# One core, two-layer hybrid decoder trunk: the SBUF tensors are allocated in another order

## The chip, the cores and the metric

The kernel runs on one core of a Trainium2 chip. The metric is the device time of one execution in microseconds; less is better. Before the change the median of three runs is 1443.9 us (1442.6 to 1444.5).

## The reference

The reference is a trunk of two layers over 512 tokens of width 1024, all in float32. Cut to what matters:

```python
for l in range(DEPTH):                                   # DEPTH = 2
    h = rmsnorm(x, norm_g[l]) * (1.0 + scale) + shift     # scale, shift, gate from silu(c) @ w_mod[l]
    parts = split_cols(h @ w_in[l])                       # 1024 -> 7200 columns
    y_a = hgrn2_mixer(...) * silu(a_g)                    # 4 heads of 128
    y_b = mla_mixer(c_q, c_kv, k_rope, ...) * silu(b_g)   # 8 heads; c_q (768) and c_kv (256) are normed first
    y_c = retention_mixer(...) * silu(c_g)                # 4 heads of 128
    merged = (sigmoid(m_a) * (y_a @ w_pa[l]) + sigmoid(m_b) * (y_b @ w_pb[l])
              + sigmoid(m_c) * (y_c @ w_pc[l]))
    x = x + gate * (merged @ w_out[l])
return rmsnorm(x, final_g)
```

## The kernel before

Everything is kept transposed: a tile is 128 features (the partitions) by 512 tokens, 2 KiB in each partition. A loop over the two layers holds one long list of steps, written out for each engine; semaphores tie the engines together.

**The stream of weights.** The weights of a layer come as 93 items of at most 128 x 1024 elements, through a ring of three slots. SP loads an item into `raw` (L548). ScalarE (ACT) copies it, rounded to the matmul format fp32r, into `w_hi` (L839). GpSimd (POOL) subtracts and puts the rest into `w_lo` (L576). The other operand of each product is likewise held as two tensors, a rounded part and a rest. So each 128x128 block of weights gives three matmuls with 512 columns, all into one accumulator in PSUM. `wh` and `wl` are the blocks that stay in the array (stationary), `hi` and `lo` the tiles that stream through it (moving):

```python
nc.tensor.matmul(dst[0:m, :], wh, hi, start=(k == 0), stop=False)
nc.tensor.matmul(dst[0:m, :], wh, lo, start=False, stop=False)
last = nc.tensor.matmul(dst[0:m, :], wl, hi, start=False, stop=(k == nk - 1))
```

These are lines 663 to 665 (`item`), and lines 648 to 650 for the first two items of a layer (`first_items`). In the rows of the profile the moving operand is named first and the stationary one second: `ps_st<-h_hi,w_hi`. There are five kinds of moving operand, chosen in `moving`:

- `h_hi`, `h_lo`: the normed input of the layer, for all columns of `w_in`. These are tensors of their own.
- `cq_hi`, `cq_lo`, `ckv_hi`, `ckv_lo` (MLA's up-projections), `y_hi`, `y_lo` (the outputs of HGRN2 and MLA, for `w_pa` and `w_pb`), `yc_hi`, `yc_lo` (retention, for `w_pc`), `mg_hi`, `mg_lo` (the merged sum, for `w_out`). These lie in the region that the stages share, the arena.

The mixers' own matmuls (scores, values, transposes, column sums) are plain float32, not fp32r.

**SBUF.** A partition of SBUF is one row of bytes. `sb(name, shape)` allocates the next tensor behind the one before. The arena is 92 KiB; `at(name, offset, ...)` places a tensor at a fixed offset from its start, and tensors of different stages lie over one another there. Every offset is a multiple of 1 KiB. Before the change the arena stands behind everything else.

**Ahead of the loop** ScalarE's queue loads 16 pieces of `w_mod_first` into `pro_w` in the arena, VectorE (DVE) folds them into `pro_acc`, and `x` is loaded by SP.

The functions and lines that the change touches:

Of the kernel before, what the change touches and what calls it, by code (L numbers as in the profile page):

```python
# [33 lines left out]
P = 128  # L34
D_MODEL, SEQ, DEPTH = 1024, 512, 2
DT = D_MODEL // P
# [344 lines left out]
def build(nc, x_t, positions, cst, decay, params_cur, params_nxt, w_stream, w_mod, w_mod_first, out_t):  # L381
    ctx = ExitStack()
    with ctx:
        def sb(name, shape, dt=F32):
            return ctx.enter_context(nc.sbuf_tensor(name, shape, dt))
# [2 lines left out]
            return ctx.enter_context(nc.semaphore(name))  # L388


        x = sb("x", [P, DT, SEQ])
        h_hi = sb("h_hi", [P, DT, SEQ], F32R)
        h_lo = sb("h_lo", [P, DT, SEQ], F32R)
        raw = sb("raw", [P, RING, SLOT])
        w_hi = sb("w_hi", [P, RING, SLOT], F32R)
        w_lo = sb("w_lo", [P, RING, SLOT], F32R)
# [20 lines left out]
        carry = sb("carry", [P, 1])  # L417
        neg_max = sb("neg_max", [P, CH])


        arena = nc.sbuf_base + (-nc.sbuf_base) % 64
        KB = 1024

        def at(name, offset, shape, dt=F32):
            return nc.alloc_sbuf_tensor_at(name, shape, dt, offset=arena + offset)


        hg_q, hg_k, hg_b = at("hg_q", 0, [P, 2, SEQ]), at("hg_k", 4 * KB, [P, 2, SEQ]), at("hg_b", 8 * KB, [P, 2, SEQ])
        hg_e, hg_x = at("hg_e", 12 * KB, [P, 2, SEQ]), at("hg_x", 16 * KB, [P, 2, SEQ])
        hg_at = (at("hg_at0", 20 * KB, [P, CH, SEQ]), at("hg_at1", 40 * KB, [P, CH, SEQ]))  # L430
        hg_kd = at("hg_kd", 28 * KB, [P, 3 * P])
        hg_qc = at("hg_qc", 64 * KB, [P, 3, 3 * P])
        hg_vt = at("hg_vt", 69 * KB, [P, SEQ])
        hg_v = at("hg_v", 71 * KB, [P, 2, CH, P])
# [22 lines left out]
        merged = at("merged", 32 * KB, [P, DT, SEQ])  # L457
        y_hi, y_lo = at("y_hi", 48 * KB, [P, CH, SEQ], F32R), at("y_lo", 56 * KB, [P, CH, SEQ], F32R)
        sigma = at("sigma", 84 * KB, [P, 3, SEQ])
        arena_end = arena + 92 * KB  # L460
        assert arena_end <= nc.sbuf_usable_end, (arena_end, nc.sbuf_usable_end)
        mg_hi, mg_lo = at("mg_hi", 0, [P, DT, SEQ], F32R), at("mg_lo", 16 * KB, [P, DT, SEQ], F32R)

        pro_w = at("pro_w", 0, [P, PRO_RING, D_MODEL])
# [1217 lines left out]
```

## Time and profile before

| | |
|---|---|
| median of 3 runs | 1443.9 us (1442.6 to 1444.5) |
| the profiled execution, its own time | 1443.96 us |
| its span in the trace | 1442.2 us |
| PE (matmul) busy | 1323.3 us, 92% |
| DVE, ACT, POOL busy | 758.0, 641.3 and 601.4 us |
| mean granted TensorE clock | 0.978 of full speed |

Matmuls overlap one another in the trace: one takes some 390 ns from start to end, while the next one starts some 230 ns after it. So a busy PE does not tell how fast the stream of matmuls runs; the distance from one start to the next does, and it is read from a list of instructions in order of time.

### The profile page before, as it was taken

What the parts mean: (1) busy time and instruction counts of PE and PEld (TensorE: products, weight loads), DVE (VectorE), ACT (ScalarE), POOL (GpSimd) and SP (SyncE); (2) the same over time, 40 slices, a digit from 0 to 9 for tenths busy, and PEclk for the clock granted to TensorE, in tenths of its full rate; (3) what the DMA queues carried; (4) which work ended last, traced back from release to release, by engine and by line L of the source; (5) the groups of instructions that cost most, each with busy time, mean ns of one, the idle gap of its engine ahead of it and who ended that gap; (6) DMA issues with size and microseconds to landing.
All of it is one profiled execution on the core that took longest, in us unless ns stands there. A gap on an engine that the chain in (4) does not pass through costs nothing.

```text
span 1442.2 us, 20431 instructions
## 1 busy us (share of the span) xinstructions
PE 1323.3 (92%) x5886; PEld 1040.6 (72%) x5886; DVE 758.0 (53%) x1174; ACT 641.3 (44%) x988; POOL 601.4 (42%) x756
## 2 busy tenths in 40 slices
PE   0389889999999999999978988999999999999996
PEld 0177677888777777778856777778877777778884
DVE  6877876533455424433337787653346541444333
ACT  2245544544455334444334555455445533444531
POOL 3243333464323444545534332346432344445451
PEclk9999999999999999999988999999999999999998
DMA  9132212244223233333323222224422223333331
GB/s 368 38 102 74 70 55 89 83 136 125 79 72 94 86 106 106 88 105 110 89 76 109 72 61 61 92 83 133 131 74 74 84 99 98 104 91 111 101 97 59
DMA packets 46057, 140.06 MB, mean 97 GB/s; under 512 B 5744, under 2 KB 5744, under 8 KB 45680
## 3 DMA queue, kind: packets, MB, share of 16 engines
q1 hardware_dynamic: 28656, 102.65, 23.6%
q10 hardware_dynamic: 17280, 35.99, 7.8%
q8 instruction: 52, 0.85, 0.2%
q14 instruction: 69, 0.57, 0.1%
HBM read 136.52 MB, written 2.10 MB: 96 GB/s over the span
## 4 chain that ended last, share of the span: by engine, by line
PE 78%; DVE 12%; issue 4%; ACT 4%; DMA 1%; ACTq 1%; DVEq 0%
PE ps_st L663 21%; PE ps_st L665 21%; PE ps_st L664 21%; PE ps_o L685 4%; PE ps_s L755 2%; PE ps_s L710 2%; PE ps_s L779 1%; PE ps_w L764 1%; DVE pro_acc L1131 1%; PE ps_misc L680 1%; DMA pro_w<-w_mod_first 1%; DVE hg_x L1340 1%; DVE h_lo L1400 1%; DVE gate_x L1190 1%; PE ps_misc L671 1%
## 5 line engine op out<-in xcount | busy, mean ns | idle before, releaser
L576 POOL TENSOR_TENSOR w_lo<-raw,w_hi 128x256 fp32r<-128x256 f32 x744 | 588.3, 822 | 793.9 <-ACT w_hi L839 793.5
L663 PE MATMUL ps_st<-h_hi,w_hi 128*128 128x512 f32 x1008 | 416.5, 413 | 0.7 <-POOL w_lo L576 0.4
L665 PE MATMUL ps_st<-h_hi,w_lo 128*128 128x512 f32 x1008 | 398.6, 395 | 0.0
L664 PE MATMUL ps_st<-h_lo,w_hi 128*128 128x512 f32 x1008 | 398.2, 395 | 0.0
L663 PEld LDWEIGHTS ps_st<-h_hi,w_hi 128*128 128x128 f32 x1008 | 193.3, 192 | 48.9 <-issue 8.3
L664 PEld LDWEIGHTS ps_st<-h_lo,w_hi 128*128 128x128 f32 x1008 | 192.7, 191 | 44.6 <-issue 6.2
L665 PEld LDWEIGHTS ps_st<-h_hi,w_lo 128*128 128x128 f32 x1008 | 192.1, 191 | 41.8
L839 ACT ACTIVATE w_hi<-raw 128x1024 fp32r<-128x1024 f32 x186 | 195.2, 1050 | 29.9 <-PE ps_st L665 27.5
L861 ACT ACTIVATE gate_t<-gate_x 128x512 f32<-128x512 f32 x80 | 50.6, 632 | 242.2 <-DVE gate_x L1190 242.2
L1190 DVE TENSOR_SCALAR gate_x<-ps_st 128x512 f32<-128x512 f32 x80 | 55.2, 690 | 193.0 <-PE ps_st L665 191.4
L710 PE MATMUL ps_s<-hg_x 128*128 128x128 f32 x384 | 54.4, 292 | 28.7 <-DVE hg_x L1340 28.7
L1538 DVE SCALAR_TENSOR_TENSOR mod_acc<-mod_w,cond,mod_acc 128x512 f32<-128x512 f32 x84 | 71.3, 848 | 10.0
L710 PEld LDWEIGHTS ps_s<-hg_x 128*128 128x128 f32 x384 | 49.9, 203 | 34.2 <-issue 19.9
L863 ACT ACTIVATE gate_t<-gate_t,cs 128x512 f32<-128x512 f32 x80 | 57.9, 724 | 2.6
L663 PE MATMUL ps_st<-y_hi,w_hi 128*128 128x512 f32 x128 | 51.1, 399 | 0.0
L664 PE MATMUL ps_st<-y_lo,w_hi 128*128 128x512 f32 x128 | 50.6, 395 | 0.0
L665 PE MATMUL ps_st<-y_hi,w_lo 128*128 128x512 f32 x128 | 50.5, 395 | 0.0
L665 PE MATMUL ps_st<-mg_hi,w_lo 128*128 128x512 f32 x128 | 50.5, 394 | 0.0
L663 PE MATMUL ps_st<-mg_hi,w_hi 128*128 128x512 f32 x128 | 50.4, 394 | 0.0
L664 PE MATMUL ps_st<-mg_lo,w_hi 128*128 128x512 f32 x128 | 50.4, 394 | 0.0
L589 PE MATMUL ps_misc<-cs,pro_acc 128*128 128x1 f32 x32 | 7.1, 352 | 46.1 <-DVE pro_acc L1131 46.1
L1256 DVE SCALAR_TENSOR_TENSOR x<-ps_st,gate,x 128x512 f32<-128x512 f32 x16 | 12.0, 750 | 63.1 <-PE ps_st L665 63.1
(233 smaller groups left out, 1987.9 us busy)
## 6 DMA issues: line engine op xcount, KB each, us to landing
raw<-w_stream SPq DMA_DIRECT2D x186, 512.0 KB, 3.6
mod_w<-w_mod ACTq DMA_DIRECT2D x96, 256.0 KB, 2.7
pro_w<-w_mod_first ACTq DMA_DIRECT2D x16, 512.0 KB, 12.7
x<-x_t SPq DMA_DIRECT2D x4, 512.0 KB, 10.5
ret_decay<-decay ACTq DMA_DIRECT2D x2, 1024.0 KB, 4.9
out_t<-o_t SPq DMA_DIRECT2D x8, 256.0 KB, 2.2
cs<-cst SPq DMA_DIRECT2D x1, 906.5 KB, 5.2
pos_i<-positions ACTq DMA_DIRECT2D x1, 256.0 KB, 7.3
```

The lines of the kernel that those rows point to most:

```text
L576: ins = nc.gpsimd.tensor_tensor(w_lo[:, i % RING, r], raw[:, i % RING, r], w_hi[:, i % RING, r].bitcast(F32), ALU.subtract)
L663: nc.tensor.matmul(dst[0:m, :], wh, hi, start=(k == 0), stop=False)
L664: nc.tensor.matmul(dst[0:m, :], wh, lo, start=False, stop=False)
L665: last = nc.tensor.matmul(dst[0:m, :], wl, hi, start=False, stop=(k == nk - 1))
L685: last = nc.tensor.matmul(dst[:, k * P:], values(k), weights[:, k, k * P:], start=(k == 0), stop=(k == CH - 1))
L710: last = nc.tensor.matmul(dst[:, r], left[:, r], right[:, r], start=True, stop=True)
L755: nc.tensor.matmul(dst[:, 0:w], mla_q[0:96, h % 2, qi * P:w], mla_kv[0:96, h % 2, 0:w], start=True, stop=False)
L839: A(w_hi[:, i % RING, 0:n], raw[:, i % RING, 0:n], ACT.Copy).then_inc(w_hi_ready, 1)
L861: A(t_n, x_n, ACT.Exp, scale=-1.0).then_inc(act_link, 1)
L863: A(t_n, t_n, ACT.Ln, bias=one).then_inc(act_link, 1)
L1190: V.tensor_scalar(gate_x[:, n % 2, :], bank[bank_of((it, 0))][:], SIG_MIN, None, ALU.max)\
L1538: ins = V.scalar_tensor_tensor(mod_acc[:], mod_w[:, n % 2, :], cond[:, k:k + 1], mod_acc[:], ALU.mult, ALU.add)
```

## The change

Only the places of the tensors in SBUF change. The list of instructions, their operands, their waits and their order are the same, word for word, on all five engines. The diff:

```diff
@@ build()
-        x = sb("x", [P, DT, SEQ])
+        KB = 1024
         h_hi = sb("h_hi", [P, DT, SEQ], F32R)
         h_lo = sb("h_lo", [P, DT, SEQ], F32R)
+        arena = nc.sbuf_base + (-nc.sbuf_base) % 64
+        sb("arena_room", [P, 92 * KB // 4 + 16])
+        x = sb("x", [P, DT, SEQ])
         raw = sb("raw", [P, RING, SLOT])
         w_hi = sb("w_hi", [P, RING, SLOT], F32R)
         w_lo = sb("w_lo", [P, RING, SLOT], F32R)
@@
         neg_max = sb("neg_max", [P, CH])
-        arena = nc.sbuf_base + (-nc.sbuf_base) % 64
-        KB = 1024
@@
-        arena_end = arena + 92 * KB
-        assert arena_end <= nc.sbuf_usable_end, (arena_end, nc.sbuf_usable_end)
```

The room for the arena is 92 KiB and 64 bytes more. The addresses in a partition that follow from the two orders, in bytes (1152 bytes are taken ahead of the first tensor in both), and their remainders by 128 and by 256, which hold for every piece of the tensor that is a multiple of 256 bytes from its start:

| tensor | before | rest by 128, by 256 | after | rest by 128, by 256 |
|---|---|---|---|---|
| `h_hi`, `h_lo` | 17536, 33920 | 0, 128 | 1152, 17536 | 0, 128 |
| the arena, 92 KiB | 133952 to 228160 | 64, 64 | 33920 to 128128 | 0, 128 |
| `x` | 1152 | 0, 128 | 128192 | 64, 192 |
| `raw`, `w_hi`, `w_lo` | 50304, 62592, 74880 | 0, 128 | 144576, 156864, 169152 | 64, 192 |
| `mod_w`, `mod_acc`, `cs` | 87168, 91264, 93312 | 0, 128 | 181440, 185536, 187584 | 64, 192 |
| `rstd`, `gate_t`, `sq_sum` | 112352, 118496, 130784 | 96, 224 | 206624, 212768, 225056 | 32, 32 |

Before the change all of the arena lies above 131072 (128 KiB), and `h`, `x`, the weights' ring and the constants below it. After it the arena and `h` lie below that address, and the weights' ring and what follows above. These two parts are called the lower and the upper half here.

## Rows read from the trace of the kernel before

**Rows 1.** The page: busy time of each engine, PE's tenths and granted clock in 40 slices
```profile
PE 1323.3 (92%) x5886; PEld 1040.6 (72%) x5886; DVE 758.0 (53%) x1174; ACT 641.3 (44%) x988; POOL 601.4 (42%) x756
...
PE   0389889999999999999978988999999999999996
...
PEclk9999999999999999999988999999999999999998
```

**Rows 2.** The page: the chain that ended last, shares by engine and by line
```profile
PE 78%; DVE 12%; issue 4%; ACT 4%; DMA 1%; ACTq 1%; DVEq 0%
PE ps_st L663 21%; PE ps_st L665 21%; PE ps_st L664 21%; PE ps_o L685 4%; PE ps_s L755 2%; PE ps_s L710 2%; PE ps_s L779 1%; PE ps_w L764 1%; DVE pro_acc L1131 1%; PE ps_misc L680 1%; DMA pro_w<-w_mod_first 1%; DVE hg_x L1340 1%; DVE h_lo L1400 1%; DVE gate_x L1190 1%; PE ps_misc L671 1%
```

**Rows 3.** Windows of the first layer: window, its length, busy us (count) of each engine, PEclk, DMA share, GB/s
```profile
70.00:240.00 170.00, 153.00 (x707) 123.58 (x707) 134.19 (x231) 85.78 (x142) 66.63 (x76) 0.94 0.26 77
240.00:300.00 60.00, 58.75 (x260) 47.04 (x259) 30.82 (x44) 30.83 (x49) 29.37 (x36) 1.00 0.33 101
300.00:365.00 65.00, 65.00 (x286) 52.98 (x285) 18.42 (x24) 26.09 (x35) 35.22 (x49) 1.00 0.42 126
365.00:500.00 135.00, 134.50 (x637) 102.10 (x636) 73.25 (x121) 67.78 (x119) 42.82 (x57) 1.00 0.28 83
500.00:620.00 120.00, 120.00 (x508) 91.28 (x507) 44.76 (x67) 49.45 (x70) 53.66 (x68) 1.00 0.33 99
620.00:745.00 125.00, 121.96 (x531) 98.54 (x530) 45.79 (x63) 48.15 (x66) 59.06 (x80) 1.00 0.32 94
```

**Rows 4.** Line 663, its instructions: count, duration in ns (min/median/max), first and last start
```profile
L663 PEld LDWEIGHTS ps_st<-h_hi,w_hi x1008: 186/188/337, 81.3 to 1376.5; 128*128 128x128 f32 x168
L663 PE MATMUL ps_st<-h_hi,w_hi x1008: 387/389/988, 81.3 to 1376.7; 128*128 128x512 f32 x168
...
L663 PE MATMUL ps_st<-y_hi,w_hi x128: 393/394/497, 298.7 to 1314.5; 128*128 128x512 f32 x128
...
L663 PE MATMUL ps_st<-mg_hi,w_hi x128: 393/394/395, 696.8 to 1427.1; 128*128 128x512 f32 x128
...
L663 PE MATMUL ps_st<-cq_hi,w_hi x96: 393/394/484, 331.7 to 1136.5; 128*128 128x512 f32 x96
...
L663 PE MATMUL ps_st<-yc_hi,w_hi x64: 393/394/395, 646.2 to 1382.3; 128*128 128x512 f32 x64
...
L663 PE MATMUL ps_st<-ckv_hi,w_hi x32: 393/394/399, 335.9 to 1137.9; 128*128 128x512 f32 x32
```

**Rows 5.** PE in order of time, matmuls with `h` moving: start us, duration us
```profile
304.32 0.39 PE L663 MATMUL ps_st<-h_hi,w_hi 128*128 128x512 f32 x1
...
305.48 0.39 PE L665 MATMUL ps_st<-h_hi,w_lo 128*128 128x512 f32 x1
305.70 0.39 PE L663 MATMUL ps_st<-h_hi,w_hi 128*128 128x512 f32 x1
...
309.78 0.39 PE L663 MATMUL ps_st<-h_hi,w_hi 128*128 128x512 f32 x1
```

**Rows 6.** The same, with `mg` moving: the first and the last of `w_out`'s 192 in layer 1
```profile
696.78 0.39 PE L663 MATMUL ps_st<-mg_hi,w_hi 128*128 128x512 f32 x1
...
741.34 0.40 PE L665 MATMUL ps_st<-mg_hi,w_lo 128*128 128x512 f32 x1
```

**Rows 7.** Line 680, plain float32 column sums, their instructions as in Rows 4
```profile
L680 PE MATMUL ps_misc<-o_sq,cs x32: 590/592/692, 134.8 to 1315.6; 128*128 128x512 f32 x32
...
L680 PE MATMUL ps_misc<-sq_sum,cs x8: 590/692/1220, 58.0 to 955.4; 128*128 128x512 f32 x8
```

**Rows 8.** Lines 791 and 685, weight loads of plain float32, as in Rows 4
```profile
L791 PEld LDWEIGHTS ps_w<-cs,mod_acc x96: 187/192/193, 179.7 to 1355.2; 128*128 128x128 f32 x96
...
L685 PEld LDWEIGHTS ps_o<-ret_sc,ret_v x64: 187/190/192, 530.7 to 1303.9; 128*128 128x128 f32 x64
```

**Rows 9.** Groups by line and form: count, busy us, mean ns, idle before and its releaser
```profile
L576 POOL TENSOR_TENSOR w_lo<-raw,w_hi 128x256 fp32r<-128x256 f32 x744 | 588.3, 822 | 793.9 <-ACT w_hi L839 793.5
...
L874 ACT ACTIVATE sigma<-gate_t 128x512 f32<-128x512 f32 x48 | 30.3, 632 | 4.8
...
L1152 DVE TENSOR_TENSOR mg_lo<-merged,mg_hi 128x512 fp32r<-128x512 f32 x16 | 10.4, 689 | 1.0
...
L944 ACT ACTIVATE sq_t<-x 128x512 f32<-128x512 f32 x16 | 10.1, 632 | 67.4 <-DVE sq_sum L1283 61.7 <-DVE x L1256 5.7
...
L1231 DVE TENSOR_TENSOR sq_sum<-sq_sum,sq_t 128x512 f32<-128x512 f32 x10 | 6.9, 689 | 28.0 <-ACT sq_t L908 28.0
```

**Rows 10.** DMA queues, 8 to 20 us: packets, MB, share of the 16 engines' time
```profile
q10 hardware_dynamic: 657, 2.43, 50.6%
q1 hardware_dynamic: 658, 2.40, 50.5%
```

## The prediction

> **What bounds the kernel now.** I read the page first: PE is busy 1323.3 of 1442.2 us, and its tenths stand at 9 nearly everywhere but at the two starts of a layer [rows 1]. The chain that ended last is PE for 78%, and 63% of it is the three matmul lines of `item` [rows 2]. The windows say where PE is the only limit: from 300 us to the end of the layer it is busy 65.00 of 65, 134.50 of 135 and 120.00 of 120 us; the loss of 3.0 us between 620 and 745 is the turn to the next layer. Only between 70 and 240 us, where HGRN2 runs beside it, does PE lose 17 of 170 us [rows 3]. The clock is not in question: it is at its upper level in all of these windows but the first, where 0.94 of it is granted [rows 3]. So what this kernel pays for is the distance from one fp32r matmul to the next, and an allocation can move the time only if that distance, or a wait in the HGRN2 stage, depends on where an operand lies.
>
> Does it? The same line, with the same weights' ring as stationary operand and the same 512 columns, shows two durations. With `h` moving the median is 389 ns; with `y`, `mg`, `cq`, `yc` and `ckv` moving it is 394 ns each time, and nearly without spread (393 to 395 for `mg` and `yc`) [rows 4]. The distances say the same more sharply. From 305.70 to 309.78 us there are 18 steps with `h` moving: 4.08/18 = 0.2267 us. From 696.78 to 741.34 us there are 191 steps with `mg` moving: 44.56/191 = 0.2333 us [rows 5, 6]. That is 6.6 ns more, and the weights, the engine and the shape are the same. What differs is the place of the moving tensor: `h` stands at a rest of 0 by 128 and in the lower half of the addresses, the arena at a rest of 64 and in the upper half (table of the change). I cannot tell from this trace which of the two it is. For the moving operand I need not: after the change the arena has the rest of `h`, by 128 and by 256, and lies in the lower half, and `h` keeps its rest and its half.
>
> **The change part by part.**
> No instruction is added, removed or moved, so each term is a count times a difference in duration.
>
> (a) Moving operands in the arena. Line 663 has 128 + 128 + 96 + 64 + 32 = 448 of them [rows 4], and lines 664 and 665 as many each: 1344. If they come down from 0.2333 to 0.2267 us that is 1344 x 0.0066 = -8.9 us. They lie in the stretches from 298 to 743 us and the same of layer 2, where PE is busy all the time [rows 3], so none of it is hidden. A part may not be had: with `h` moving too, the first steps behind a change of operand or a wait are longer (304.32 to 305.48 us, 5 steps, 0.232 each [rows 5]). The 16 items of MLA's up-projections begin behind a step of the attention, so some 6 of each one's 24 may gain nothing: 16 x 6 x 0.0066 = +0.6. On the other side the slow first steps of `h` behind an arena item would go (5 x 0.005 us, some 15 times: -0.4). Sum -8.7.
>
> (b) The stationary operands. `w_hi` and `w_lo` go from a rest of 0 by 128 to 64, and from the lower to the upper half. The fp32r stream has no row with them elsewhere. The nearest rows are weight loads. One takes 188 ns in the stream [rows 4], against a step of 227, so some 39 ns are in hand; a penalty of 6.6 ns as for a moving operand would lie inside that. So the lower bound is 0. The upper bound is that the penalty shows in full wherever it does not now: then all 3120 matmuls with `h` (1008 x 3 [rows 4] and 96 of the first items) go to 0.2333, 3120 x 0.0066 = +20.6 us, less the quarter that runs at 0.23 already (6 of 24 steps, [rows 5]): +15.5. I take 0, because the load has room and because the difference that is seen goes with the moving tensor's name and never with the slot of the ring.
>
> (c) Plain float32 matmuls. The column sums with `o_sq` (arena) and with `sq_sum` (below the arena, rest 96) both have a shortest duration of 590 ns [rows 7]. A weight load from `mod_acc`, below, takes 187 to 193 ns and one from `ret_v`, in the arena, 187 to 192 [rows 8]. I take 0; the bound is some 2 ns on about 1400 of them, 3 us to either side, half of it hidden.
>
> (d) ScalarE and VectorE. The same activation of 128x512 takes 632 ns from `x` (rest 0, lower half) and from `gate_t` into `sigma` (rest 96 into the arena) [rows 9]. VectorE takes 689 ns for two tiles of 512 both at a rest of 96 (`sq_sum`) and in the arena (`mg_lo`) [rows 9]. No sign of an address: 0.
>
> (e) GpSimd. Its four subtractions of an item read `raw` and `w_hi` and write `w_lo`, all three of which move. There is no row for them elsewhere. But GpSimd idles 793.9 us in front of them, all of it waiting for ScalarE [rows 9]; 6 ns on each of 744 would be 4.5 us of busy time and nothing in the end: 0. If they took 10% longer (82 ns), the ring would still be ahead: 3.3 us of work per item against some 5.4 us of matmuls (24 x 0.227).
>
> (f) DMA. Between 8 and 20 us queue 1 fills `x` and `raw` (rest 0) and queue 10 `pro_w` (rest 64 by 128), side by side: 2.40 MB for 50.5% and 2.43 MB for 50.6% [rows 10], the same price to 1%. So swapping their rests costs nothing; in the prologue, which waits for `pro_w` and where VectorE and GpSimd get in each other's way, I allow 1 us to either side.
>
> The sum against the profiled execution: 1443.96 - 8.7 = 1435.3 us. That execution is at the median of the runs (1443.9), so the forecast for the median is **1435.2 us**; this case's own range is 1433.5 to 1437.5, from (a) without its losses and (f) on one side to half of (c) on the other.
>
> A page speaks against any effect. The Trainium skill, "TensorE: Matmul & The Clock Gate", section "Back-to-back issue gap", gives the gap as columns over clock plus 2.5 ns and knows no address in it. By it the time would not change. The row says that the gap is 227 for one tensor and 233 for others at one column count, so here the measurement decides. The same section says that in a stream of weight loads and matmuls the spacing is set by both; that speaks for the rival below. "Step-by-step: what each phase is for" on the same page gives the moving and the stationary operand a read port each, which speaks against it; no row here shows the ports.
>
> **The rivals.**
> *The stationary operand counts as well: slower.* The place is lines 648 to 650 and 663 to 665 with `h` moving. Today both operands are at a rest of 0 for `h`, and they differ for the arena. After the change moving and stationary differ everywhere (rests 128 and 192 by 256; today's `y` and `w_hi` are 64 and 128, the same difference). If the longer step comes from that difference, or if each misplaced operand costs a step of 6.6 ns, `h` rises to 0.2333 and the arena stays there: +15.5 us as in (b), some of it taken by the HGRN2 stage's waits, 1459 us. For it: the step with `h` moving needs some six matmuls to settle at 0.2267 [rows 5], which looks like two streams finding their distance rather than a fixed price per address. Against it: the 39 ns of room, and that weight loads themselves take the same time wherever they read [rows 8]. It decides from the point where the step with `h` rises by more than 1344/2340 of the arena's gain, that is by 3.8 ns.
>
> *No effect: 1444.* The arena's tensors would have to be slow for another reason than their place, say by what wrote them or what runs beside them. `mg` is written by ScalarE and VectorE as `h` is, and the steps are 0.2333 in a stretch without any mixer beside it, so I see little for it.
>
> *Only a part: 1439 or so.* The step with the arena moving would stop midway, if two conditions added up, the rest and the half, and one of them were undone by what moved up with the weights.
>
> **How the numbers follow.** Moving operand alone: 0.58. The stationary one as well: 0.28. No effect, or changes that cancel: 0.08. A part: 0.06. About 0.2% (2.9 us) is what a measurement of this kernel can tell from no change. Faster takes the first and the last, 0.64; slower the second with a little of the third, 0.28; the rest, 0.08, is within 0.2%. The two signs share most of the chance, so the range reaches from the likeliest case to the rival: 1433 to 1460, with 1433.5 to 1437.5 for the likeliest case alone.
>
> **What would show it.** Line 663 in the profile after: a median of 389 ns for `y`, `mg`, `cq`, `yc`, `ckv` and a step of 0.2267 for `mg` show (a) right. 389 ns for `h` as before shows (b) right; 394 for `h` shows the rival, and 394 for all of them its full form. A weight load longer than 188 with `h` still at 0.2267 would show the room of 39 ns used. GpSimd's mean of 822 ns and the packets' shares answer to (e) and (f). The prediction is wrong if the 512-column step with `h` moves at all, or if PE begins to wait for `w_lo`.

## The result, and the profile after

The change makes the kernel slower: 1455.94 us (median of 6 runs, 1454.78 to 1456.57) against 1443.63 us (6 runs, 1441.55 to 1444.5), a ratio of 1.0088 with a 95% interval of 1.0076 to 1.0099. The forecast was 1435.2 us and faster. The time lies in the forecast's range, at the rival that had 0.28.

The page after, busy times, with its span of 1454.8 us (before: [rows 1]):

```profile
span 1454.8 us, 20431 instructions
...
PE 1338.1 (92%) x5886; PEld 1041.6 (72%) x5886; DVE 756.3 (52%) x1174; ACT 641.4 (44%) x988; POOL 601.5 (41%) x756
...
PEclk9999999999999999999988999999999999999998
```

PE is busy 14.8 us longer with the same 5886 matmuls, at the same granted clock; no other engine moved by more than 2 us. The windows, with columns as in [rows 3], show the same: PE is as busy as before, with fewer matmuls in the same stretch (499 against 508 between 500 and 620 us).

```profile
300.00:365.00 65.00, 65.00 (x282) 52.44 (x281) 18.94 (x25) 26.46 (x35) 35.31 (x49) 1.00 0.41 123
...
500.00:620.00 120.00, 120.00 (x499) 89.99 (x499) 43.93 (x66) 47.72 (x67) 53.71 (x68) 1.00 0.34 99
```

Line 661 is what was line 663 ([rows 4]): count, duration in ns (min/median/max), first and last start.

```profile
L661 PEld LDWEIGHTS ps_st<-h_hi,w_hi x1008: 186/188/337, 81.0 to 1389.5; 128*128 128x128 f32 x168
L661 PE MATMUL ps_st<-h_hi,w_hi x1008: 392/394/988, 81.1 to 1389.7; 128*128 128x512 f32 x168
...
L661 PE MATMUL ps_st<-y_hi,w_hi x128: 393/394/503, 300.2 to 1326.4; 128*128 128x512 f32 x128
...
L661 PE MATMUL ps_st<-mg_hi,w_hi x128: 393/396/398, 703.0 to 1440.1; 128*128 128x512 f32 x128
```

With `h` moving the duration went from 389 to 394 ns; with the arena's tensors it did not come down; the weight load is at 188 ns as before. The distances, from PE in order of time:

```profile
636.57 0.40 PE L662 MATMUL ps_st<-h_lo,w_hi 128*128 128x512 f32 x1
...
651.27 0.39 PE L662 MATMUL ps_st<-h_lo,w_hi 128*128 128x512 f32 x1
...
703.02 0.40 PE L661 MATMUL ps_st<-mg_hi,w_hi 128*128 128x512 f32 x1
...
741.52 0.39 PE L661 MATMUL ps_st<-mg_hi,w_hi 128*128 128x512 f32 x1
```

63 steps with `h` in 14.70 us are 0.2333 us each (0.2267 before, [rows 5]), and 165 steps with `mg` in 38.50 us are 0.2333 as before [rows 6]. So `h` became as slow as the arena, instead of the arena as fast as `h`. A mean hides a pattern: before the change the steps with `mg` are 232 to 235 ns each, after it they alternate between some 231 and 236 ns, with the same mean. So a single step proves little here, and a step is always given as a mean over many.

**Where the 12.3 us are.** The first matmul with `y` starts 1.5 us later than before, the first with `mg` 6.2 us later, the last with `mg` in line 661 13.0 us later (1440.1 against 1427.1, [rows 4]). Ahead of the first `y` lie 672 matmuls with `h`. They gave 1.5 us, 2.2 ns each: this is the HGRN2 stage, where PE also waits, and a longer step there can be partly taken out of a wait. Up to the first `mg` come 888 more with `h`, which gave 4.7 us, 5.3 ns each, less than 6.6 because the first steps behind a change of operand or a wait were longer than 226.7 already: over all steps with `h` of less than 260 ns the mean goes from 228.0 to 233.3. The second layer repeats both (+2.1 and +4.7 us), which makes 13.0 in this one profiled execution.

### The profile page after: what moved, and what is told of

It is laid out like the page before. It is cut to its first block, busy times and chain, and to the rows that moved or that the text cites. A ratio compares the mean times of both kernels' runs of the same rounds, so it can differ in the third digit from the quotient of the medians.

```text
span 1454.8 us, 20431 instructions
## 1 busy us (share of the span) xinstructions
PE 1338.1 (92%) x5886; PEld 1041.6 (72%) x5886; DVE 756.3 (52%) x1174; ACT 641.4 (44%) x988; POOL 601.5 (41%) x756
## 4 chain that ended last, share of the span: by engine, by line
PE 79%; DVE 12%; issue 4%; ACT 4%; DMA 1%; ACTq 1%; DVEq 0%
PE ps_st L661 21%; PE ps_st L662 21%; PE ps_st L663 21%; PE ps_o L683 4%; PE ps_s L753 2%; PE ps_s L708 2%; PE ps_s L777 1%; PE ps_w L762 1%; DVE pro_acc L1129 1%; PE ps_misc L678 1%; DMA pro_w<-w_mod_first 1%; DVE hg_x L1338 1%; DVE h_lo L1398 1%; DVE gate_x L1188 1%; PE ps_misc L669 1%
## 5 line engine op out<-in xcount | busy, mean ns | idle before, releaser
L661 PE MATMUL ps_st<-h_hi,w_hi 128*128 128x512 f32 x1008 | 421.4, 418 | 0.0
L662 PE MATMUL ps_st<-h_lo,w_hi 128*128 128x512 f32 x1008 | 402.7, 400 | 0.0
L1043 ACT ACTIVATE mla_p<-ps_s,neg_max 128x512 f32<-128x512 f32 (+1 forms) x64 | 32.1, 526 | 29.1 <-DVE neg_max L1495 29.1
```

Source lines behind the costliest of these rows:

```text
L1043: A(mla_p[:, qi % 2, 0:w], src[:, 0:w], ACT.Exp, bias=neg_max[:, qi:qi + 1]).then_inc(free[bank_of(s)], 1)
```

## The experiments

The start addresses of all pieces of a tensor have one rest by 256 bytes. In what follows **d** is the rest of the moving tensor less the rest of the weights' ring, by 256. Before the change d is 0 for `h` and -64 for the arena (64 - 128); after it -64 for both (128 - 192). A step is the mean distance from start to start in a stretch without a wait. `sb("pad", [P, n])` puts 4 x n bytes ahead of what follows.

**1. The change without its 64 bytes**

```diff
-        sb("arena_room", [P, 92 * KB // 4 + 16])
+        sb("arena_room", [P, 92 * KB // 4])
```

> The changed order, but the room for the arena is 92 KiB exactly, so x, the weights' ring and all behind it stand 64 bytes lower. Moving operands and weights then all have a rest of 0 by 128 (128 by 256), with the weights still in the upper half and the moving operands in the lower. Theory A (the step is long, 0.2333 us, where the rests of moving and stationary operand differ by 64): every fp32r step 0.2267, about 1435 us. Theory B (a rest of 64 at either operand makes it long): the same, 1435. Theory C (the halves: short only where both operands are in the same half): all steps stay at 0.2333, 1456. Theory D (upper half for either operand is slow): 1456.

Measured: 1435.24 us (1433.97 to 1435.5), ratio to before 0.9942 (0.9925 to 0.9958). The new order is kept, only what stands behind the arena moves down by 64 bytes, and the slower kernel becomes one that is faster than before. Its line 661, and PE in order of time:

```profile
L661 PE MATMUL ps_st<-h_hi,w_hi x1008: 387/389/988, 81.2 to 1369.7; 128*128 128x512 f32 x168
...
L661 PE MATMUL ps_st<-mg_hi,w_hi x128: 389/389/389, 693.3 to 1418.7; 128*128 128x512 f32 x128
```
```profile
693.27 0.39 PE L661 MATMUL ps_st<-mg_hi,w_hi 128*128 128x512 f32 x1
...
734.07 0.39 PE L661 MATMUL ps_st<-mg_hi,w_hi 128*128 128x512 f32 x1
```

180 steps in 40.80 us are 0.2267, for `mg` too. The weights stand in the upper half here with a step of 0.2267, so a half is not what costs: theories C and D are out, A and B stand. The slow first steps of `h` behind an arena item are gone as well:

```profile
303.44 0.39 PE L661 MATMUL ps_st<-h_hi,w_hi 128*128 128x512 f32 x1
...
304.57 0.39 PE L663 MATMUL ps_st<-h_hi,w_lo 128*128 128x512 f32 x1
```

These are the first 5 steps with `h` behind `y`, 1.13/5 = 0.226 us each, where they were 0.232 before the change ([rows 5]).

**2. The kernel before, the arena moved by 64 bytes**

```diff
-        arena = nc.sbuf_base + (-nc.sbuf_base) % 64
+        arena = nc.sbuf_base + (-nc.sbuf_base) % 64 + 64
```

> The order of before, with the arena moved up by 64 bytes and nothing else: rests 0 by 128 for moving and stationary alike, halves as before. Theories A and B: the arena's matmuls come down from 0.2333 to 0.2267, h stays, about 1443.6 - 8.7 = 1435 us. Theories C and D: no change, 1443.6.

Measured: 1434.32 us (1433.88 to 1435.81), ratio 0.9939 (0.9923 to 0.9956). Order and weights are those of before, the arena is still in the upper half. `mg` steps at 0.2267, and its duration is that of `h` before:

```profile
L663 PE MATMUL ps_st<-mg_hi,w_hi x128: 389/389/389, 693.1 to 1418.1; 128*128 128x512 f32 x128
```

Here the arena and the weights differ by 256 in their rests by 512, and it makes no difference.

**3. As experiment 1, with everything 64 bytes higher**

```diff
+        sb("pad", [P, 16])
         h_hi = sb("h_hi", [P, DT, SEQ], F32R)
```

> As the first kernel of this call, with 64 bytes ahead of everything: all moving operands and all weights at a rest of 64 by 128 (192 by 256). Theory A: the rests are equal, so all steps are 0.2267, 1435 us, the same as the first kernel. Theory B: both operands are at 64, so all steps are 0.2333 or, if the two add up, 0.2400: 1456 or 1475. Theory C: 1456.

Measured: 1433.84 us (1432.93 to 1434.41), ratio 0.9935 (0.9919 to 0.9952). All three stand at a rest of 192 by 256, and all step at 0.2267:

```profile
L662 PE MATMUL ps_st<-mg_hi,w_hi x128: 389/389/389, 692.0 to 1416.6; 128*128 128x512 f32 x128
```

Theory B is out, A stands. So it is not the rest of one operand, whichever: it is the difference.

**4. The kernel before with d = 64 for `h` and 128 for the arena**

```diff
         x = sb("x", [P, DT, SEQ])
+        sb("pad0", [P, 16])
...
+        sb("pad1", [P, 48])
         raw = sb("raw", [P, RING, SLOT])
...
-        arena = nc.sbuf_base + (-nc.sbuf_base) % 64
+        arena = nc.sbuf_base + (-nc.sbuf_base) % 256
```

> The order of before with h moved up by 64 bytes (rest 192 by 256) against weights at 128, the difference of h and weights being +64 where it was -64 for the arena in both kernels; the arena is at a rest of 0 by 256, 128 away from the weights. Theory A by 128: h long, arena short, 1456 - 8.7 = 1447 us. If the sign of the difference counts (only -64 by 256 is long): h short and arena short, 1435. If the arena's difference of 128 is long or longer too: 1456 or more. Theory B: h long, arena short, 1447.

Measured: 1444.13 us (1443.05 to 1447.75, 10 runs), ratio 1.001 (1.0 to 1.002). PE in order of time, the first and last of 63 steps with `h` and of 166 with `mg`:

```profile
631.04 0.39 PE L666 MATMUL ps_st<-h_lo,w_hi 128*128 128x512 f32 x1
...
645.46 0.39 PE L666 MATMUL ps_st<-h_lo,w_hi 128*128 128x512 f32 x1
...
696.61 0.39 PE L665 MATMUL ps_st<-mg_hi,w_hi 128*128 128x512 f32 x1
...
735.19 0.40 PE L666 MATMUL ps_st<-mg_lo,w_hi 128*128 128x512 f32 x1
```

That is 0.2289 for d = 64 and 0.2324 for d = 128. None of the cases that had been expected came. The step with `h` lies between short and long, so +64 and -64 are not alike; the arena's at 128 is nearly the long one. The time falls between the 1435 and the 1447 us of the first two cases.

**5, 6. The same at a finer pitch.** As experiment 4 with these numbers:

```diff
+        sb("pad0", [P, 8])       # 6: 24
+        sb("pad1", [P, 56])      # 6: 40
+        arena = nc.sbuf_base + (-nc.sbuf_base) % 256 + 96      # 6: + 32
```

> d is the rest by 256 of the moving operand less that of the weights. Known so far: d = 0 gives a step of 0.2267, d = -64 0.2333, d = +64 about 0.229, d = 128 about 0.232 us. Here h has d = +32 and the arena d = -32. If the step goes by pieces of 64 bytes and counts the piece in which an operand starts: h as at 0 (weights start at 128, h at 160: the same piece of 64), arena as at -64, 1443 us. If it goes smoothly with d: h between 0.2267 and 0.229, arena near 0.230: 1440 us. If any d other than 0 is as bad as -64: 1456. Theory B (a rest of 64 by 128 at either operand) no longer applies, since no operand has that rest: 1435.

> h has d = +96, the arena d = -96. Smooth: h between the steps of +64 and 128 (0.229 to 0.232), arena between those of 128 and -64 (0.232 to 0.233), 1449 us. By pieces of 64: h as at +64, arena as at 128, 1445 us. A step below 0.2267 at any d would show that d = 0 is not the best place.

Measured: 1455.13 us (1454.18 to 1455.47, ratio 1.0078, 1.0062 to 1.0095) for d = 32 and -32, and 1457.86 us (1456.99 to 1459.14, ratio 1.0097, 1.008 to 1.0113) for d = 96 and -96. 32 bytes on either side cost the full 6.6 ns: d = 0 is a narrow place, not the bottom of a slope. First and last of 66 steps with `h` at d = 32 (experiment 5), then of 63 with `h` at 96 and of 134 with `mg` at -96 (experiment 6):

```profile
635.09 0.40 PE L667 MATMUL ps_st<-h_hi,w_lo 128*128 128x512 f32 x1
...
650.49 0.40 PE L667 MATMUL ps_st<-h_hi,w_lo 128*128 128x512 f32 x1
```
```profile
638.04 0.40 PE L667 MATMUL ps_st<-h_hi,w_lo 128*128 128x512 f32 x1
...
652.74 0.40 PE L667 MATMUL ps_st<-h_hi,w_lo 128*128 128x512 f32 x1
...
704.41 0.39 PE L665 MATMUL ps_st<-mg_hi,w_hi 128*128 128x512 f32 x1
...
735.80 0.39 PE L667 MATMUL ps_st<-mg_hi,w_lo 128*128 128x512 f32 x1
```

They give 15.40/66 = 0.2333, 14.70/63 = 0.2333 and 31.39/134 = 0.2343 us. Experiment 5 came as its third case had it (1456). Experiment 6 fits neither of its cases (1449 and 1445): both were worked out from the 228.9 of d = 64, which is an exception among long steps.

**7. The low weights apart from the high ones**

```diff
+        sb("pad1", [P, 64])
         raw = sb("raw", [P, RING, SLOT])
         w_hi = sb("w_hi", [P, RING, SLOT], F32R)
+        sb("pad2", [P, 16])
         w_lo = sb("w_lo", [P, RING, SLOT], F32R)
...
+        arena = nc.sbuf_base + (-nc.sbuf_base) % 256 + 192
```

> w_lo alone is 64 bytes further: h has d = 0 against w_hi and -64 against w_lo, the arena +64 and 0. Of three matmuls two load w_hi and one w_lo. While the second one (w_hi, h_lo) streams, the block of w_lo for the third is loaded. If the step is long because of the load that runs beside the stream, the second matmul's step is the long one; if because of the weights that are in the array, the third one's. If only the average counts, all three rise to about 0.229. In each case h gains a third of the 12.3 us that it lost in the change: about +4, and the arena a third of the difference between d = 0 and +64 less: 1441 us.

Here `w_hi` stands at a rest of 128 and `w_lo` at 192; d is 0 for `h` with `w_hi`, -64 for `h` with `w_lo`; the arena is at 192, so it is 64 and 0 there. Measured: 1446.02 us (1444.87 to 1448.98, 10 runs), ratio 1.0023 (1.0013 to 1.0032); 1441 had been expected. Matmuls and weight loads in order of time:

```profile
641.38 0.39 PE L666 MATMUL ps_st<-h_lo,w_hi 128*128 128x512 f32 x1
641.38 0.19 PEld L667 LDWEIGHTS ps_st<-h_hi,w_lo 128*128 128x128 f32 x1
641.61 0.40 PE L667 MATMUL ps_st<-h_hi,w_lo 128*128 128x512 f32 x1
641.61 0.19 PEld L665 LDWEIGHTS ps_st<-h_hi,w_hi 128*128 128x128 f32 x1
```

The load for the next matmul starts with the present matmul, so `w_lo` (L667) is loaded under the second one (L666). With `h`, the steps from the start of the first, second and third matmul of a block are 228.4, 229.1 and 235.9 ns (means of the 16 blocks between 636.3 and 647.4 us, from starts to the ns, finer than the lines print). The long one is that of the matmul whose own weights are displaced, not the one under which `w_lo` is loaded. Where a block with `h` ran without a wait, the third step is the longest in 817 of 906 blocks; in experiment 6, where all three pairs have one d, it is in 362 of 904. But its neighbours do not come back to 226.7. The three make 693 ns, where 2 x 226.7 + 233.3 = 687 would be the sum of separate prices. With `mg`, where the pair of `w_lo` has d = 0 and the two others 64, they are 230.4, 228.7 and 227.5. That shows nothing of the pairs, for in experiment 8 `mg` has 229.2, 231.7 and 225.8 with d = 64 for all three: a steady pattern of steps can keep time with the block. So with `h` at d = 0 and -64 a matmul's own pair matters most, and something is carried over to its neighbours; for other d this is not shown.

**8. The mirror of experiment 4**: d = 128 for `h`, 64 for the arena

```diff
+        sb("pad0", [P, 32])
+        sb("pad1", [P, 32])
+        arena = nc.sbuf_base + (-nc.sbuf_base) % 256 + 192
```

> h has d = 128 and the arena d = +64: the roles of the kernel with h at +64 and the arena at 128 are exchanged. If d alone decides, the arena's step is 0.229 and that of h 0.232: 1443.6 + 0.59 x 3120 x 0.0053 - 1344 x 0.004 = 1448 us. If instead the tensor or the half of the addresses decides, h keeps the step of 0.229 that it had there and the arena 0.232: 1444.

Measured: 1449.83 us (1449.07 to 1450.1), ratio 1.0044 (1.0027 to 1.006). The steps change places: 0.2324 with `h` (634.13 to 648.77 us, 63 steps), 0.2289 with `mg` (34.56 us, 151 steps):

```profile
700.04 0.39 PE L665 MATMUL ps_st<-mg_hi,w_hi 128*128 128x512 f32 x1
...
734.60 0.40 PE L666 MATMUL ps_st<-mg_lo,w_hi 128*128 128x512 f32 x1
```

For these two values the step goes with the place and not with the tensor that has it.

| d, bytes | step, ns | from |
|---|---|---|
| 0 | 226.7 | `h` before; all in 1, 2, 3 |
| 64 | 228.9 | `h` in 4, `mg` in 8 |
| 128 | 232.4 | `mg` in 4, `h` in 8 |
| 32, -32, 96 | 233.3 | `h` in 5, `mg` in 5, `h` in 6 |
| -64 | 233.3 | `mg` before, all after the change |
| -96 | 234.3 | `mg` in 6 |

Only d = 0 and d = -64 were measured with the weights at two rests (128 and 192), and there the step depends on the difference alone. The other rows all have the weights at 128; that they hold elsewhere is not shown.

**9. bf16 operands in the four output projections**, 416 columns, four values of d

```diff
+                            if it[0] in ("wo", "pa", "pb", "pc"):
+                                c0 = {"wo": 0, "pc": 32, "pb": 64, "pa": 96}[it[0]]
+                                wh = wl = ident_bf[:, 0:m]
+                                hi = lo = mov_bf[:, c0:c0 + 416]
```

> The order of before, but the matmuls of the four output projections read a constant bf16 tensor and the bf16 identity in place of their operands, 416 columns, at the same d: 0 in w_out, +64 in w_pc, 128 in w_pb, -64 in w_pa. The projections are left out; only their time is looked at. Half as many bytes are read per column. If the dependence belongs to the rate at which fp32r reads SBUF, the four steps are equal, near 0.176 us. If it belongs to any pair of moving tile and weight block, they differ by 2 to 7 ns as with fp32r.

Measured (one run): 1389.51 us. PE in order of time: an item of `w_pa`, one of `w_pc`, and a stretch of `w_out`, whose starts in `mov_bf` lie 192, 64 and 0 bytes from its own:

```profile
298.48 0.35 PE L668 MATMUL ps_st<-mov_bf,ident_bf 128*128 128x416 bf16 x1
...
302.54 0.34 PE L670 MATMUL ps_st<-mov_bf,ident_bf 128*128 128x416 bf16 x1
...
634.78 0.35 PE L668 MATMUL ps_st<-mov_bf,ident_bf 128*128 128x416 bf16 x1
...
638.84 0.34 PE L670 MATMUL ps_st<-mov_bf,ident_bf 128*128 128x416 bf16 x1
...
686.55 0.34 PE L670 MATMUL ps_st<-mov_bf,ident_bf 128*128 128x416 bf16 x1
...
697.10 0.34 PE L670 MATMUL ps_st<-mov_bf,ident_bf 128*128 128x416 bf16 x1
```
```profile
L668 PEld LDWEIGHTS ps_st<-mov_bf,ident_bf x320: 95/98/98, 298.5 to 1372.3; 128*128 128x128 bf16 x160
```

4.06/23 = 0.1765 us both times, with each item's longer first steps in it, and 10.55/60 = 0.1758; the items of `w_pb` (128) step alike. No sign of d in bf16. But not only the bytes per column changed: a weight load takes 98 ns here and not 188, so the room beside it is 78 ns and not 39, and every matmul loads the same block. Which of the three frees the step from d is not shown. The Trainium skill, "TensorE: Matmul & The Clock Gate", section "Back-to-back issue gap", gives columns over 2.4 GHz plus 2.5 ns for a matmul by itself, 175.8 ns for 416 columns. This stream of loads and matmuls agrees with it, 175.8 ns. For 512 columns that formula would give an estimate of 215.8, and the fp32r steps above are 10.9 to 18.5 ns longer.

**10. fp32r at 416 columns**, on the kernel of experiment 2

```diff
+                            if it[0] in ("wo", "pa", "pb", "pc"):
+                                c0 = {"wo": 0, "pc": 16, "pb": 32, "pa": 48}[it[0]]
+                                hi, lo = hi[:, c0:c0 + 416], lo[:, c0:c0 + 416]
```

> The kernel with the arena shifted (d = 0 everywhere), but the fp32r matmuls of the four output projections stream only 416 of the 512 columns, starting at column 0 in w_out, 16 in w_pc, 32 in w_pb and 48 in w_pa: d = 0, +64, 128 and -64 bytes. The other 96 columns of each product are left out. At 512 columns the steps are 0.2267, 0.2290, 0.2324 and 0.2333 us, of which 0.2133 is the columns at 2.4 GHz. If the rest is a cost per matmul, the steps are 0.1733 plus the same 13.3, 15.7, 19.1 and 20.0 ns: 0.187, 0.189, 0.192, 0.193. If it goes with the columns: 0.184, 0.186, 0.189, 0.190. If the weight load bounds the step instead, all four are near 0.188 and equal.

Measured (one run): 1394.93 us. First and last matmul of an item of `w_pa` (d = -64), of one of `w_pb` (d = 128), of one of `w_pc` (d = 64), and of a stretch of `w_out` (d = 0), then the weight loads of `w_out`:

```profile
296.70 0.35 PE L666 MATMUL ps_st<-y_hi,w_hi 128*128 128x416 f32 x1
...
301.00 0.35 PE L668 MATMUL ps_st<-y_hi,w_lo 128*128 128x416 f32 x1
...
612.62 0.35 PE L666 MATMUL ps_st<-y_hi,w_hi 128*128 128x416 f32 x1
...
617.00 0.35 PE L668 MATMUL ps_st<-y_hi,w_lo 128*128 128x416 f32 x1
...
634.41 0.35 PE L666 MATMUL ps_st<-yc_hi,w_hi 128*128 128x416 f32 x1
...
638.74 0.35 PE L668 MATMUL ps_st<-yc_hi,w_lo 128*128 128x416 f32 x1
...
685.05 0.35 PE L667 MATMUL ps_st<-mg_lo,w_hi 128*128 128x416 f32 x1
...
716.88 0.35 PE L668 MATMUL ps_st<-mg_hi,w_lo 128*128 128x416 f32 x1
```
```profile
L666 PEld LDWEIGHTS ps_st<-mg_hi,w_hi x128: 186/188/191, 680.5 to 1378.6; 128*128 128x128 f32 x128
```

4.30/23 = 0.1870, 4.38/23 = 0.1904, 4.33/23 = 0.1883 and 31.83/169 = 0.1883 us. The stretch of `w_out` leaves out its first 22 steps, three of which are 234 to 293 ns long; the mean of all 191 would be 0.1894. The other three items of `w_pb` in this layer, with the same d = 128, begin with one step of 302 ns and then step at 0.1867. So one d gives 186.7 and 190.4 ns, and the spread within a value is as large as that between the values. Nearest is the third case of the expectation, "near 0.188 and equal", if not quite equal: a weight load takes 188 ns, the step is 187 to 190 ns, and one load starts as the last one ends. With the loads back to back this run can tell neither whether the price of d belongs to a matmul or to its columns, nor which d is the best at 416 columns. A count between 416 and 512, where the load still has room, would be needed, and was not run.

**11. The old order with the new rests**: the kernel before, the weights and all behind them 64 bytes higher

```diff
+        sb("pad1", [P, 16])
         raw = sb("raw", [P, RING, SLOT])
```

> The order of before, halves as before, with 64 bytes ahead of raw: the weights' ring goes to a rest of 192 by 256 and the arena behind it to 128, the same rests as in the changed kernel, d = -64 for h and for the arena. If the rests are all that the change did: every fp32r step 0.2333, 1456 us, the time of the changed kernel. If the order or the halves did a part of it: less.

Measured: 1456.53 us (1455.25 to 1457.27), ratio 1.0095 (1.0078 to 1.0112). Its line 664:

```profile
L664 PE MATMUL ps_st<-h_hi,w_hi x1008: 388/394/988, 81.2 to 1388.6; 128*128 128x512 f32 x168
...
L664 PE MATMUL ps_st<-mg_hi,w_hi x128: 393/395/399, 703.2 to 1439.0; 128*128 128x512 f32 x128
```

This is the whole effect of the change without the change: the first `mg` starts at 703.2 us, after the change at 703.0. The order of the tensors and the halves add nothing that can be seen (1.0095 against 1.0088, with intervals of under 0.002 to either side); the 64 bytes do it.

## Why the prediction was wrong

- **What bounds the kernel: right.** PE's fp32r stream does, and its distance from start to start is what the allocation moved. The 6.6 ns between `h` and the arena were read rightly. Not quite right is "Only between 70 and 240 us": from 240 to 300 us PE is busy 58.75 of 60 us [rows 3]; nothing hangs on it.
- **Step (b) failed**, "The stationary operands", taken as 0. It was worth +12.3 us with an upper bound of +15.5; the full penalty came on every matmul with `h`, and what is missing to 15.5 lies in the HGRN2 stage, where 672 of them gave 1.5 us. Two reasons had been given for 0. The room of 39 ns beside a weight load is real (the load is at 188 ns in both kernels), but the price does not show as loading time. The other, that the difference "goes with the moving tensor's name and never with the slot of the ring", proves nothing: all three slots, and `w_hi` and `w_lo`, had the same rest, so the trace of before could not show it.
- **Step (a) failed with it**, for it rests on "For the moving operand I need not", that is, on the place of the moving operand alone. The arena's d was -64 before and -64 after, and its step stayed 233.3. Its size was right, for the case it described: experiment 2, which brings the arena to d = 0 and nothing else, gave 1434.32 against 1444.06, -9.7 us, where -8.7 had been worked out. Its small term of -0.4, for the slow first steps of `h` behind an arena item, is borne out by the 0.226 us of experiment 1.
- **The rival** had the mechanism in its first form: "If the longer step comes from that difference". Experiment 3 decides for it against its second form, a price for each misplaced operand: there both are at 192 and nothing is paid. It said 1459; measured 1455.9. It had 0.28, half of what was given to the forecast. The sign that it named, the steps before `h` settles behind `y` [rows 5], is gone where `y` and `h` have the same d (experiment 1), so it was a true one, and should have weighed more than an argument about room.
- **(c) to (f): right.** Granting them 0 was correct: GpSimd's subtractions are at 822 ns and idle in front of them as before, and the two DMA queues pay the same with their rests exchanged, between 8 and 20 us.

```profile
L574 POOL TENSOR_TENSOR w_lo<-raw,w_hi 128x256 fp32r<-128x256 f32 x744 | 588.4, 822 | 807.1 <-ACT w_hi L837 806.2
```
```profile
q1 hardware_dynamic: 660, 2.41, 51.0%
q10 hardware_dynamic: 659, 2.44, 50.9%
```

- **Open.** Why d matters is not shown. In the trace the load of the next weights runs beside the present matmul, and experiment 7 puts the price, for d = -64, mostly on a matmul's own pair with some of it carried on; whether two reads meet at one place in SBUF, or the start of a stream is put off to some boundary, no run here tells apart. Nor is it shown whether the price depends on the column count (the loads fill the step in experiment 10), or what in experiment 9 takes it away.

The fastest of those measured are the versions with d = 0 for both kinds of moving operand: 1433.8 to 1435.2 us in experiments 1 to 3, 0.6% under the kernel before and 1.4 to 1.5% under the change.

## What to carry to other kernels

Where a stream of fp32r matmuls is the bound, write down the start addresses of the moving and of the stationary tensors by 256 bytes and keep them equal (shown for 512 columns), with the padding stated in the code: 64 bytes decide 0.6% (experiment 2) to 1.4% (experiment 1 against the change) of this kernel. A reordering of an allocation is two changes in one, places and rests; try the rests alone first. And where all of one operand's tensors share a property, a trace cannot say that the property costs nothing.

## What was not expected of the hardware

- The distance of fp32r matmuls with 512 columns depends on the difference of the operands' start addresses by 256 bytes: 226.7 ns at 0, 233.3 at 32 bytes to either side, 228.9 at +64 against 233.3 at -64, up to 234.3 at -96. For 0 and -64, moving both operands by the same 64 bytes or to another side of 128 KiB did not change it; the other values were measured with the weights at one rest.
- The same mean can come of different patterns: steps of 232 to 235 ns, or 231 and 236 in turn (both d = -64).
- At 416 columns, where a step of 187 to 190 ns is as long as the weight load of 188, no order by d is left. In bf16, at 416 columns and with loads of 98 ns, it is 175.8 to 176.5 ns wherever the operands start.
- The durations of the instructions show it only in part (389 against 394 ns, 1.3%, where the step rises by 2.9%), and the weight loads not at all.
